# One block of programs for the four branches' stages, and a lead of four tiles for the first of two row blocks

## The reference, cut to what matters

```python
h = rms_norm(x, norm_mix_pre)
proj = h @ w_in                       # split into the inputs of four branches
o_a = rms_norm(gated_delta_rule(...), dn_norm) * silu(dn_z)      # delta net, chunks of 64
o_b = block_sweep_attention(q, k, v, scale, None)                # latent attention
o_c = rms_norm(gla_chunked(...), gla_norm) * silu(gla_g)         # gated linear
o_d = block_sweep_attention(fox_q, fox_k, fox_v, ..., forget_cum) # forgetting attention
merged = sum(sigmoid(h @ w_gate[i] + b_gate[i]) * (o[i] @ w_branch_up[i]) for i in range(4))
x = x + rms_norm(merged @ w_out, norm_mix_post)
u = relu(rms_norm(x, norm_mlp_pre) @ w_mlp_in)
x = x + rms_norm((u * u) @ w_mlp_out, norm_mlp_post)
```

## Time and profile before

| | |
|---|---|
| median of 3 runs | 2688.21 us (2688.07 to 2688.27) |
| the profiled execution | 2687.03 us, its span 2685.2 us |
| TensorE busy | 2592.3 us, 97% of the span, 14276 matmuls |
| DVE, ACT, POOL busy | 1649.9, 1143.6, 162.0 us |
| mean granted TensorE clock | 0.994 of full speed |
| branches' stages | 38.8 to 1072.7 us |
| merged rows, MLP rows | 1170 to 1268 us, 1817 to 1923 us |

### The profile page before, as it was taken

One profiled execution on the slowest core, in us unless ns is written; L12 is line 12 of the kernel. 1 busy time (PEld: TensorE's weight loads), 2 busy tenths in 40 slices (PEclk: granted clock), 3 DMA queues, 4 the chain that ended last, 5 costly groups with the idle time before them and its releaser, 6 DMA issues.

```text
span 2685.2 us, 34981 instructions
## 1 busy us (share of the span) xinstructions
PE 2592.3 (97%) x14276; PEld 2049.4 (76%) x14276; DVE 1649.9 (61%) x2139; ACT 1143.6 (43%) x1688; POOL 162.0 (6%) x290
## 2 busy tenths in 40 slices
PE   7999999999999998999999999999999999999999
PEld 6867777666776866778888878887876788888777
DVE  4375453444344455874887767756557799963854
ACT  5462222243433544643455555344478722224231
POOL 0102210000100000100121100000000000000000
PEclk9999999999999999999999999999999999999999
DMA  4323311110312211661343468863211121113341
GB/s 161 118 83 68 60 42 53 66 37 32 114 57 96 75 49 35 222 250 47 114 166 141 161 235 311 270 222 123 90 39 39 53 78 55 55 56 114 110 168 53
DMA packets 104577, 289.76 MB, mean 108 GB/s; under 512 B 11241, under 2 KB 16137, under 8 KB 104417
## 3 DMA queue, kind: packets, MB, share of 16 engines
q1 hardware_dynamic: 81120, 208.01, 22.8%
q0 software_dynamic: 23296, 79.51, 9.2%
HBM read 225.54 MB, written 61.93 MB: 107 GB/s over the span
## 4 chain that ended last, share of the span: by engine, by line
PE 42%; DVE 5%; ACT 2%; issue 1%; DMA 1%; DVEq 0%; ACTq 0%
PE psum L289 16%; PE psum L3492 16%; PE psum L3788 3%; PE psum L5163 2%; PE psum L338 1%; DVE lru_convolved L4362 1%; DMA weights_raw_second<-in_w_mlp_back 1%; PE psum L354 0%; DVE pool_arena L4890 0%; PE psum L3846 0%; DVE lru_gated_input L4373 0%; PE psum L4239 0%; DVE weights_parts L256 0%; DMA weights_raw<-in_gain_rows 0%; PE psum L4445 0%
## 5 line engine op out<-in xcount | busy, mean ns | idle before, releaser
L289 PE MATMUL psum<-mixer_in,weights_parts 128*128 128x512 f32 x2016 | 469.7, 394 | 2.2 <-DVE weights_parts L256 2.2
L289 PEld LDWEIGHTS psum<-mixer_in,weights_parts 128*128 128x128 f32 x2016 | 378.2, 188 | 94.4 <-issue 9.7
L484 PE MATMUL psum<-hidden,weights_parts 128*128 128x512 f32 x1536 | 403.7, 410 | 11.0 <-ACT early_gate L508 4.5
L484 PEld LDWEIGHTS psum<-hidden,weights_parts 128*128 128x128 f32 x1536 | 283.5, 191 | 86.6 <-issue 17.9
L289 PE MATMUL psum<-hidden,weights_parts 128*128 128x512 f32 x1104 | 253.7, 392 | 5.5 <-PEq L909 2.8
L3492 PE MATMUL psum<-mixer_in,weights_parts 128*128 128x512 f32 x1104 | 255.5, 391 | 0.0
L3492 PE MATMUL psum<-mlp_in,weights_parts 128*128 128x512 f32 x1080 | 251.4, 392 | 1.8 <-DVE weights_parts L3342 1.6
L256 DVE TENSOR_TENSOR weights_parts<-weights_raw,weights_parts 128x1024 fp32r<-128x1024 f32 (+2 forms) x110 | 107.5, 977 | 231.8 <-ACT weights_parts L240 231.7
L289 PEld LDWEIGHTS psum<-hidden,weights_parts 128*128 128x128 f32 x1104 | 207.0, 188 | 52.0 <-issue 6.9
L3492 PEld LDWEIGHTS psum<-mixer_in,weights_parts 128*128 128x128 f32 x1104 | 207.3, 188 | 45.4
L3492 PEld LDWEIGHTS psum<-mlp_in,weights_parts 128*128 128x128 f32 x1080 | 202.3, 188 | 48.1 <-DVE weights_parts L3342 4.2
(11 more groups left out here) (569 smaller groups left out, 4084.1 us busy)
## 6 DMA issues: line engine op xcount, KB each, us to landing
weights_raw<-in_w_in SPq DMA_DIRECT2D x69, 512.0 KB, 3.6
hidden_sums_scratch<-y POOLq DMA_DIRECT2D x84, 256.0 KB, 2.7
weights_raw<-in_w_gate SPq DMA_DIRECT2D x32, 512.0 KB, 3.7
gate_scratch<-early_gate SPq DMA_DIRECT2D x64, 256.0 KB, 2.2
gate<-gate_scratch POOLq DMA_DIRECT2D x32, 512.0 KB, 4.4
weights_raw<-in_w_mlp_back SPq DMA_DIRECT2D x30, 512.0 KB, 5.4
weights_raw_second<-in_w_mlp_back SPq DMA_DIRECT2D x30, 512.0 KB, 4.7
mod_weights<-in_mod_w POOLq DMA_DIRECT2D x48, 256.0 KB, 3.6
```

The costliest lines, as they stand in the source:

```text
L289: mm = nc.tensor.matmul(c.psum[:, bank + h, 0:cols], c.parts[:, s, wp, at], moving(k, xp, h), start=(n < halves), stop=(n >= halves * (3 * ...
L484: mm = nc.tensor.matmul(c.psum[:, bank, :], c.parts[:, s, wp, at], self.hidden[:, k, xp, h * HALF:(h + 1) * HALF], start=(k == 0 and n == ...
```

## The change

The stages from the small projections to the forgetting attention share one block. `begin_block` opens it, and the stages' `with c.block()` then give them that block, so that no barrier stands between them. In its place `c.enter()` notes at each stage how many steps each engine will have made by then, and `c.after(eng, ...)` makes one engine wait for the other engines' step counts; `c.after_units` waits for the copies of a gemm's units. On TensorE these waits stand behind a first portion of filler in four stages. A gemm in the shared block counts as joined: TensorE waits for the readers of the banks it will write, and for the split weights. The sums of squares in the latent inputs go to other banks, and the first waits only for two of the three units. One branch instruction per stage and engine stays, where there were two.

`FIRST_TWO` becomes `first_two(ahead)`: 4 for the two row stages, 2 (as before) in the second layer's `mixer_out`.

```diff
+    def begin_block(self):
+        self.held = self.nc.Block()
+        self.open_block = self.held.__enter__()
+    def block(self):
+        return nullcontext(self.open_block) if self.open_block else self.nc.Block()
+    def enter(self):
+        self.entered = dict(self.base)
+    def after(self, eng, *engines):
+        for name in engines:
+            if self.entered[name]:
+                eng.wait_ge(self.steps[name], self.entered[name])
+    def after_units(self, eng):
+        for sem, name in ((self.act_done, "gemm_act"), (self.dve_done, "gemm_dve")):
+            if self.entered[name]:
+                eng.wait_ge(sem, self.entered[name])
...
+    in_front = block is None and c.open_block is not None and not begun
+    block = block or c.open_block
+    joined = block is not None and not begun if joined is None else joined
...
         def high(u, w=D):
-            if u >= 2:
-                act.wait_ge(c.unit_done, self.u0 + u - 1)
+            act.wait_ge(c.unit_done, self.u0 + u - 1)
...
     (gated_linear_inputs; forgetting_inputs alike)
             @block.sync
+                c.after(sp, "pe", "act", "vec")
+                c.after_units(sp)
             @block.tensor
+                early.pe(p, e + 4)
+                c.after_units(p)
+                c.after(p, "act", "vec")
                 turn_values(p)
...
     (latent_inputs)
+                p.wait_ge(c.act_done, projected - 2)
                 for h in range(NH):
                     for n in range(2):
-                        last = mm(c.psum[:, h, :], c.ones[:], sq[:, n, cols], ...
+                        last = mm(c.psum[:, 2 + h, :], c.ones[:], sq[:, n, cols], ...
                 last.then_inc(pes.step("sums"), 1)
+                early.pe(p, e + 4)
+                p.wait_ge(c.act_done, projected)
...
     (attend; attend_by_pairs alike)
+                early.pe(p, upto(0))
+                c.after(p, "act", "vec")
                 score(0)
...
     (every stage, on each engine that needs it)
-        with nc.Block() as block:
+        with c.block() as block:
+                c.after(a, "pe", "act", "vec")
...
+            c.begin_block()
             small = c.sb("small_projections", [P, 2, S], ctx=inner)
...
+            c.end_block()
...
-FIRST_TWO = [(0, 0), (0, 1), (1, 0), (1, 1)] + [(b, k) for k in range(2, KT - 2) for b in range(2)] + [
-    (b, k) for b in range(2) for k in range(KT - 2, KT)]
+def first_two(ahead):
+    return [(0, 0), (0, 1), (1, 0), (1, 1)] + [
+        (b, k) for k in range(2, KT - ahead) for b in range(2)] + [
+        (b, k) for b in range(2) for k in range(KT - ahead, KT)]
```

More of the change, by code:

```diff
@@ L245, in epilogue @@
                 if act_epilogue:
+                    if in_front and u == 0:
+                        c.after(act, "pe", "act", "vec")
                     act.wait_ge(c.unit_done, u + (u0 + 1))
@@ L879, in project_and_modulate, with load @@
 def project_and_modulate(nc, c, t, name, first, n, hidden, proj, then, sums, finished=None):
+    c.enter()
     with ExitStack() as ctx:
         modulation = Modulation(nc, c, t, name, sums, ctx)
+        def load(pool):
+            c.after(pool, "pe", "act", "vec")
+            modulation.load(pool)
         def on_dve(v, q, j):
@@ L922, in _ @@
             def _(v):
+                c.after(v, "pe", "act", "vec")
                 early.dve(v, e)
@@ L1577, in _ @@
                 mm = nc.tensor.matmul
+                c.after(p, "vec")
                 spread_first_rows()
@@ L5185, in _ @@
         own(0)
-        for b, k in FIRST_TWO:
+        for b, k in first_two(2):
             if b == 0:
```

52 lines of the change are left out of this document (42 added, 10 removed).

## The result

The changed kernel takes 2670.05 us (median of 4, 2667.53 to 2671.73) against 2688.14 for the kernel before. The ratio is 0.9935, 95% interval 0.9917 to 0.9952. The forecast was 2665.4 in a range of 2658 to 2673: the direction and the range held, and the gain was overestimated by 4.6 us. The profiled span is 2667.0 us instead of 2685.2, 18.2 less. TensorE is still busy 97% of it, so the time is again made of TensorE's waits and of stretches in which it runs at half its clock (slow spells, for short).

The account below looks back on a forecast made before the run. TensorE, busy 97% of the span, bounds the kernel, so time is won only where it idles or runs at half speed. Branches' stages 17.1 plus rows' lead 5.7 gave 22.8 us: 2665.4 us, range 2658 to 2673.

Parts of the forecast that it names:

- rival (d): Stage entries: the crossing costs a branch, not a barrier; up to 42 us against 22.8 won, 2707 us; chance 0.02.
- Joined gemms, forgetting inputs, gated chunks, gated inputs: Branch stages: gemm entries save 1.4, 1.3 and 2.8 us, forgetting inputs 1.35, gated chunks 0.9, gated inputs 0.2.
- Delta inputs: Delta net's inputs: TensorE starts 1.4 us earlier, gain 0.3, the rest becoming a longer wait for DVE's low norms.
- Last read and its slow spell: Delta net's last read: wait of 2.4 us shrinks, gain 1.4; slow spell behind counted at 1.0, between 0 and 2.2.
- Latent inputs: Latent inputs' entry: sums over the first two units run at once, then filler; gain 2.3 us, set by DVE's reciprocals.
- Latent attention: Latent attention's entry: filler goes ahead of the scores, DVE starts at 557.3 instead of 558.17; gain 1.1 us.
- Forgetting attention: Forgetting attention's entry: same filler move where there was nearly no wait, DVE starts at 958.4 instead of 957.38; loss 1.0 us.
- Gated tokens to channels: Gated tokens-to-channels entry: filler starts at 841.2, the turn comes at 850.45 instead of 853.97; gain 3.5 us.
- The rows' lead: Merged and MLP rows: with 4 the first row block ends 12 matmuls sooner; gains 2.8 and 2.9 us, sum 5.7.
- (b): Slow spells left in the forecast go, at the last read and behind matmuls with few rows; 2661 us; chance 0.10.
- (c): Row stages: the lead finds its weights late or frees the bank for nothing, giving 0 to 1; 2670 us; chance 0.06.
- Rival (a): New waits of about 1 us bring slow spells of 1.7 us at three or four places; 2671 us; chance 0.14.

Follow-up runs that it names:

- e10: e6 with nine of the delta inputs' 24 filler matmuls taken forward into the waits for the last squares and low norms; 2658.17 us.
- e3: Changed kernel with a 128x1 exponential ahead of the wait for the first maxima in both attentions, so the table loads early; 2666.27 us.
- e4: Changed kernel with the twelve filler matmuls of both attentions put back behind the first scores, no barrier; 2665.83 us.
- e1: The block alone: changed kernel with the rows' lead back at two tiles in both row stages, joined entries kept; 2673.5 us.
- e9: Changed kernel with twelve of the delta inputs' 24 filler matmuls moved into the middle of the sixteen matmuls of 8 rows; 2669.87 us.
- e2: The lead alone: kernel before, barriers kept, with the rows' lead of four tiles in both row stages; 2682.95 us.
- e7: e6 with the filler ahead of the first scores, as in the change; 2663.23 us.
- e5: Changed kernel with both the early exponential table load and the filler behind the first scores, in both attentions; 2662.31 us.
- e6: e5 with the attention masks and gate_up also loaded during the delta inputs, into tiles of their own; 2659.72 us.
- e8: e6 with the lead of four tiles also in the second layer's closing rows stage; 2661.13 us.
- e11: e10 with the lead of four tiles also in the second layer's closing rows stage; 2658.62 us.

## Why the prediction was right in its range and 4.6 us off

The mechanism held: the barriers' waits went and nothing was paid in their place for the crossing. The branches' stages gained 10.7 us of the 17.1 forecast, though, 6.4 too little. That the profiled execution came out only 4.6 short is owed to the second layer's missing spell, 1.8 us that the change did not earn (of the other executions in the median there is no trace to tell); the rows' lead gave what was forecast, and the stretches of unchanged code on either side of the merged rows lost 1.1 and gained 1.1. By the prediction's own steps:

- **Crossing without a barrier costs nothing, rival (d).** Right. No PEq wait but 0.3 us, and the block alone gained 14.3 us. Branches that cost 0.76 us or more each would have taken all of it.
- **Joined gemms, forgetting inputs, gated chunks, gated inputs.** Right within the profile's grain: from the attention's first values to the gated gate 2.0 gained (1.5 forecast), from there to the gated turn 4.7 (4.4). The gate waits 0.90 for its DMA (1 forecast). The 21.6 us of waits at entries left out one, 0.7 at the delta net's tokens; the gain counted there, 0.3, did not rest on it.
- **Delta inputs, the first step mis-sized.** The sum had 2.0 us gained by the chunks, the profile 0.1. The prediction let the earlier start of 1.4 turn into a longer wait, but kept the 1.4 of the gemm in front as won. ACT and DVE set the pace here: TensorE's wait at L1250 grew from 0.26 to 1.19, so that of the 2.2 won ahead 1.1 was left at the matmuls of 8 rows (from 182.74 to 181.61), and the spell there doubled. Over the nine joined kernels without e10's edit the first chunk's keys are turned at 208.0 on average, over the two with barriers at 208.8: 0.8 gained is the better estimate, 1.2 too little.
- **Last read and its slow spell.** The wait went from 2.37 to 1.06 as worked out (1.3 gained, 1.4 forecast). The spell was counted at 1.0 of at most 2.2; it went wholly. The window of 430 to 440 us has a granted clock of 0.66 before and 1.00 after, 6.8 us at half speed. The first 1.7 of them fell into the wait, so it had cost 2.6, and 1.6 more was won than counted: from the last read to the latent inputs' sums the kernel gained 6.6, where 5.0 was forecast.
- **Latent inputs.** Right: 8.0 gained at their sums and at their end, 8.4 forecast, the shortfall before it made good by the spell.
- **Latent attention, the step that failed.** Forecast +1.1, measured -2.5. The prediction put the filler ahead of the scores and asked only when DVE could start: 557.3, that is 0.1 behind the end of the scores. It took the mask as loaded ("earlier than that, since SP no longer waits for the weight split") and ACT's table load as free. The mask came 0.7 behind the scores' end, the load took 1.3 more, and behind the long wait came 3.4 us at half clock. What that cost can be read: from the first turn to the first values it is 4.6 us in the four kernels with this spell and 3.0 in the nine without, 1.6. Together 3.6, and 3.6 were missing.
- **Forgetting attention, the same step.** Forecast -1.0. From the gated turn to the merge the kernel lost 1.5 where 1.75 was to be won, 3.3 too little: 1.3 of it the load, the rest within the 6.8 us at half clock behind the wait. That distance was 218.8 us before and 220.3 after; it is 216.6 in e3 and 214.1 in e4. Here too chance has a part. Ahead of the scores, behind eight matmuls of one row (L2230), a spell of 3.4 us stands in eight of the thirteen profiles, before and after among them, and not in e1, e9, e3, e4 and e5. e1 and e9 have the changed kernel's code here and take 219.0 and 218.9, so it is they that e3 and e4 are to be compared with: about 2.3 and 4.9 less.
- **Gated tokens to channels.** Right: TensorE waits 1.59 (1.35 forecast).
- **The rows' lead.** Right in both stages, 2.9 and 2.9 (2.8 and 2.9). In whole runs it shows as 4.8 (e2) and 3.5 (the changed kernel against e1), within their spread.
- **Rivals (b) and (c).** Of (b) one half came true, the last read's spell. (c) is refuted by e2.
- **Rival (a), new waits bring slow spells, 2671.** It named the time (1 us off, nearer than the forecast) and part of the cause. It is shown for the latent attention. In the window of 545 to 561 us the clock is 0.89 after and in e1, e4 and e9, where TensorE waited 3.2, 3.0, 2.0 and 3.0 us for the first probabilities, and 1.00 in the other seven joined kernels, where it waited 1.7 (e3), 1.1 (e7), 0.9 (e5) or not at all. (The wait of 2.31 in the earlier trace rows, with twelve filler matmuls 0.4 us behind it, had brought none, so the wait's length alone doesn't decide.) In the forgetting attention it fits: 6.8 us at half clock behind the wait of 2.79 (after, e1, e9), none where the wait is 0.39 (e4) or 0 (e5, e6, e8, e10, e11), but 3.4 and 6.8 behind the same 1.43 in e3 and e7. For the delta inputs e10 refutes it, and behind the waits at the gated turn (1.6) no joined kernel has a spell, behind those at the gated gate (0.5 to 1.3) one has (e5).

```profile
545.00:561.00 16.00, 12.37 (x55) 9.32 (x54) 5.88 (x15) 6.16 (x18) 0.00 (x0) 0.89 0.18 60
```
```profile
545.00:561.00 16.00, 13.91 (x77) 10.60 (x76) 6.72 (x18) 6.25 (x19) 0.00 (x0) 1.00 0.22 71
```

(The first is the changed kernel, the second e3.)

Open stays why the matmuls of 8 rows are followed by 3.4 us at half clock in the kernels with barriers and by 6.8 in all others. Neither the waits (e10) nor the filler's place (e9) changed it. Open, too, is why the spell ahead of the forgetting attention's scores comes in one execution and not in another with the same code.

The experiments lead to a kernel that beats both: e10, the changed kernel with the early table load, the scores ahead of the filler, the small loads early and the filler taken forward in the delta inputs. It takes 2658.17, 11.9 less than the changed kernel and about 30 less than the one before (ratio 0.9889).

## What to carry to other kernels

When a barrier goes, look at what it let the engines do for nothing: a table load, a small transfer issued with nothing large close ahead of it. Each of them must be given a place of its own before the first data wait, with a tiny activation for the table and a tile of its own for the constant. Keep cover work between the request and the first use of a result, not ahead of the request. And credit an earlier start only as far as the stage that receives it is bound by the engine that starts earlier.

## What the runs showed of the hardware

- A table load can carry its activation's waits. The same load cost nothing where it stood behind the entry's barrier and 1.4 to 1.5 us of TensorE's time per attention where it stood behind the first maximum; an activation of 128x1 ahead (0.20 us) moved it. The Trainium skill ("ScalarE: Activation LUTs", What ACT_TABLE_LOAD costs) gives about 1283 ns for it, and the rows agree with 1.28 each. It adds a drain of about 1380 ns. None is seen here, neither where ACT was idle before (load at 550.80, activation at 552.09) nor where it was at work: a cast ends at 143.03, the load starts at 143.04 and its activation at 144.34, and 35 of the 47 loads after the change stand like that. Here the measurement decides: 1.28 us and no more.
- The same 64 KB mask took 1.8 us from issue to use in both attentions before (issued 2.8 us behind a weight transfer of 512 KB in the first, with no other transfer near in the second) and 2.9 to 3.3 in the six joined kernels that issue it 1.3 us behind such a transfer. That the transfer is the cause was not tried by itself.
- TensorE's clock fell with no idle time at all: in e10 it is busy 16.00 of 16 us from 179 to 195 us, at a granted clock of 0.79; the clock fell during the last two of sixteen matmuls of 8 rows, and in e6 in their middle:

```profile
179.00:195.00 16.00, 16.00 (x60) 12.25 (x59) 12.27 (x13) 5.12 (x8) 3.81 (x11) 0.79 0.27 91
```

- A slow spell can be chance. One and the same code had a spell of 3.4 us in some executions and none in others (the second layer near 2050 us in eleven of thirteen profiles, the forgetting inputs in eight of thirteen), 1.3 to 1.8 us of time each. A distance of one profile that runs across such a place cannot be read finer than that.
